# Modulation vectors computed up front by TensorE, or summed up by VectorE inside the other stages

## The chip, the cores and the metric

The kernel runs on one core of one Trainium2 chip. The metric is the time of one execution on the device in microseconds (us). The numbers of the trace come from one profiled execution, whose span is counted from its first instruction to its last.

## What is computed

Two transformer layers over 256 latent tokens `x` and 256 context tokens `ctx`, width D = 1024, everything in float32. Each layer first makes six modulation vectors of length D for each of two streams, one from the vector `c` (latent) and one from `c_ctx` (context):

```python
for i in range(DEPTH):                                   # 2 layers
    mod_l = (silu_c @ mod_w[i] + mod_b[i]).reshape(B, 1, N_MOD, D_MODEL)     # mod_w[i]: 1024 x 6144
    mod_c = (silu_cc @ mod_w[i] + mod_b[i]).reshape(1, N_MOD, D_MODEL)
    sh1, sc1, gt1, sh2, sc2, gt2 = [mod_l[:, :, s] for s in range(N_MOD)]
    u_l = rmsnorm(lat, norm_g[i, 0]) * (1 + sc1) + sh1
    ...  # layer 0: mLSTM mixer, layer 1: HGRN2 mixer; y_l
    lat = lat + gt1 * rmsnorm(y_l, norm_g[i, 1])
    u_l = rmsnorm(lat, norm_g[i, 2]) * (1 + sc2) + sh2
    lat = lat + gt2 * rmsnorm(ffn(u_l), norm_g[i, 3])    # layer 0: dense SwiGLU, layer 1: 8 experts, top 2
    ...  # layer 0 does the same for the context stream with csh1 ... cgt2
```

Shift and scale 1 are needed at the start of a layer, gate 1 only after the mixer, shift and scale 2 before the feed-forward part, gate 2 at the end. One layer's `mod_w` has 25 MB, so the 24 loads of 2 MB for both layers move 50 MB.

## The kernel before

The program is a list of stages, `order`. Each is one block with its own instruction stream for each engine, and all engines meet in a barrier at its end, so the times of the stages add up. The stages are: `setup` (small vectors, masks), `modulation(0)`, `norm_in` n0 (squares, scaling, 32 transposes of the tokens, then shift and scale), `mlstm_in` (projections), `mlstm_heads` (16 turns: 8 heads, 2 directions), `mixer_out`, `norm_in` n1, `feed_forward`, `modulation(1)`, `norm_in` n2, `hgrn_in` (projections), `hgrn_state`, `hgrn_pairs`, `hgrn_values`, `mixer_out`, `norm_in` n3, `routing`, `experts`, `finish`.

Weights come through `WeightStream`, a ring of `RING` slots of 2 MB. SyncE (SP) issues the load for unit n once the unit RING before it has been read for the last time (`release`). All waits of an engine are taken in the order of its instructions, so an instruction that waits holds back all that stand behind it on that engine.

Matrix products are made with each float32 operand split in two parts: ScalarE (ACT) copies a piece of 128x1024 weights to the high part, VectorE (DVE) subtracts to get the low part (`split_high`, `split_low`), and TensorE (PE) makes three matmuls of each pair. In `mlstm_in`, `hgrn_in` and `feed_forward` the pieces are double-buffered: piece p+2 is split once TensorE has done piece p. A piece in `mlstm_in` or `feed_forward` is 24 matmuls of 512 columns. In `mlstm_in` the first eight pieces (r = 0 to 7) each have a convolution of three VectorE instructions behind their split (the lines with `junk`), and after r = 3 `scan` has six instructions.

`modulation` reads `mod_w` through the same ring in 12 units of 512 columns. Each is split by ScalarE and VectorE, multiplied by TensorE with the four columns `c_parts` as the stationary operand (16 matmuls of 512 columns a unit), and the row is then either turned into columns (`mod_cols`, used as factors for each partition) or spread over the partitions (`gate`). Nothing else of the program runs beside it.

In `mlstm_heads`, for each turn n, `weigh(n)` has four VectorE instructions into `u_area`, which wait for ScalarE's exponentials; GpSimd then masks, and TensorE's `values(n)` (20 matmul records) follows. `finish(n)` is four VectorE instructions behind them. For each new head (even n) TensorE's `scores` waits until the `weigh` of the odd turn before it is done, and the exponentials wait for the `spread_m` behind `scores`.

## Time and profile before

| | before |
|---|---|
| median of 3 runs | 2219.05 us (2218.1 to 2224.69) |
| span of the profiled execution | 2219.4 us |
| TensorE busy | 1969.2 us, 89% |
| VectorE busy | 1394.1 us, 63% |
| ScalarE busy | 1112.6 us, 50% |
| DMA | 409.11 MB, mean 184 GB/s |

The busy shares are means over stages that are limited by different things. Since a barrier ends each stage, the profile is read stage by stage: first how long each takes and which engine fills it, then what one operation costs in it. The barriers of the trace put the stages at 18.3 to 120.0 us (`modulation(0)`), 120.0 to 135.4 (n0), 135.4 to 290.0 (`mlstm_in`), 290.0 to 392.4 (`mlstm_heads`), 392.4 to 469.8 (`mixer_out`), 485.4 to 863.0 (`feed_forward`), 863.0 to 956.0 (`modulation(1)`) and 972.5 to 1175.9 (`hgrn_in`).

### The profile page before, as it was taken

How to read it: one execution, taken by the hardware profiler on the slowest of the kernel's cores; microseconds unless marked ns; L12 is line 12 of the kernel's file. 1: busy time of each engine (PE TensorE's matmuls, PEld its weight loads, DVE VectorE, ACT ScalarE, POOL GpSimd, SP SyncE). 2: the span in 40 equal slices, each digit the busy share in tenths (PEclk: the TensorE clock that was granted, in tenths of full speed). 3: DMA queues.
4: the chain of work that ended last, by engine and by line, in shares of the span. 5: the costliest groups of instructions: out<-in, count | busy, mean ns of one | idle time of the engine just before them, and what ended most of it. 6: DMA issues, size and time to landing. Idle time of an engine off the chain costs nothing. (4 is left out here: it accounts for less than half of the span.)

```text
span 2219.4 us, 26725 instructions
## 1 busy us (share of the span) xinstructions
PE 1969.2 (89%) x10092; PEld 1615.5 (73%) x10092; DVE 1394.1 (63%) x1531; ACT 1112.6 (50%) x1244; POOL 110.5 (5%) x117
## 2 busy tenths in 40 slices
PE   5979988659999997869996675999999999999996
PEld 1247866548888874248895665989899898989895
DVE  5545234553233336745545844888888888888887
ACT  5433332343232225643234434677777777777765
POOL 1000012000000000000004800000000000000000
PEclk9879999879999998979998786999999999999998
DMA  9612210113232314822240004999999999999994
GB/s 328 233 60 104 76 39 1 38 38 114 76 113 76 114 57 172 310 88 94 76 152 1 1 1 149 323 348 324 345 329 348 325 348 319 354 320 336 335 331 175
DMA packets 254248, 409.11 MB, mean 184 GB/s; under 512 B 6575, under 2 KB 160327, under 8 KB 254055
## 3 DMA queue, kind: packets, MB, share of 16 engines
q1 hardware_dynamic: 254184, 408.23, 52.8%
q8 instruction: 43, 0.70, 0.1%
q14 instruction: 21, 0.17, 0.0%
HBM read 407.16 MB, written 1.05 MB: 184 GB/s over the span
## 5 line engine op out<-in xcount | busy, mean ns | idle before, releaser
L2002 DVE TENSOR_TENSOR w_low<-e_ring,w_high 128x1408 fp32r<-128x1408 f32 (+2 forms) x384 | 617.4, 1622 | 102.6 <-ACT w_high L1939 99.4
L1939 ACT ACTIVATE w_high<-e_ring 128x1408 fp32r<-128x1408 f32 (+2 forms) x384 | 528.7, 1382 | 214.7 <-PE ps L1852 212.2
L1850 PE MATMUL ps<-w_high,list_h 128*128 128x352 f32 x1024 | 338.1, 330 | 17.7 <-DVE w_low L2002 16.3
L1852 PE MATMUL ps<-w_high,list_l 128*128 128x352 f32 x1024 | 330.1, 322 | 0.0
L1851 PE MATMUL ps<-w_low,list_h 128*128 128x352 f32 x1024 | 329.3, 322 | 0.0
L1217 DVE TENSOR_TENSOR fw_low<-ring,fw_high 128x1024 fp32r<-128x1024 f32 x66 | 80.9, 1225 | 233.8 <-ACT fw_high L1183 233.8
L1850 PEld LDWEIGHTS ps<-w_high,list_h 128*128 128x128 f32 x1024 | 192.9, 188 | 26.4 <-DVE w_low L2002 25.5
L1183 ACT ACTIVATE fw_high<-ring 128x1024 fp32r<-128x1024 f32 x66 | 70.0, 1060 | 254.7 <-PE ps L1136 168.1
L1851 PEld LDWEIGHTS ps<-w_low,list_h 128*128 128x128 f32 x1024 | 193.7, 189 | 0.3
L1852 PEld LDWEIGHTS ps<-w_high,list_l 128*128 128x128 f32 x1024 | 192.9, 188 | 0.0
L1850 PE MATMUL ps<-w_high,hid_h 128*128 128x512 f32 x352 | 140.4, 399 | 5.4 <-DVE hid_l L2068 5.4
L1134 PE MATMUL ps<-u_high,fw_high 128*128 128x512 f32 x352 | 137.7, 391 | 6.7 <-DVE fw_low L1217 6.7
L1852 PE MATMUL ps<-w_high,hid_l 128*128 128x512 f32 x352 | 137.5, 391 | 0.0
L1136 PE MATMUL ps<-u_high,fw_low 128*128 128x512 f32 x352 | 137.4, 390 | 0.0
L1135 PE MATMUL ps<-u_low,fw_high 128*128 128x512 f32 x352 | 137.4, 390 | 0.0
L1851 PE MATMUL ps<-w_low,hid_h 128*128 128x512 f32 x352 | 137.3, 390 | 0.0
L387 ACT ACTIVATE u_high<-ring 128x1024 fp32r<-128x1024 f32 x96 | 98.5, 1050 | 65.7 <-PE ps L359 42.5
L419 DVE TENSOR_TENSOR u_low<-ring,u_high 128x1024 fp32r<-128x1024 f32 x96 | 111.5, 1218 | 9.5 <-ACT u_high L387 9.3
L594 DVE TENSOR_TENSOR h_part<-ring,h_part 128x1024 fp32r<-128x1024 f32 x40 | 49.0, 1225 | 79.0 <-ACT h_part L588 78.9
L588 ACT ACTIVATE h_part<-ring 128x1024 fp32r<-128x1024 f32 x40 | 42.3, 1057 | 100.9 <-PE ps L1320 100.9
L358 PE MATMUL ps<-u_high,c_parts 128*4 128x512 f32 x192 | 84.6, 441 | 6.9 <-DVE u_low L419 6.9
L359 PE MATMUL ps<-u_low,c_parts 128*4 128x512 f32 x192 | 85.0, 443 | 0.0
(323 smaller groups left out, 3631.7 us busy)
## 6 DMA issues: line engine op xcount, KB each, us to landing
e_ring<-in_e_w_gu_dram SPq DMA_DIRECT2D x128, 1408.0 KB, 8.0
ring<-in_mod_w_dram SPq DMA_DIRECT2D x24, 2048.0 KB
e_ring<-in_e_w_down_dram SPq DMA_DIRECT2D x32, 1536.0 KB, 7.2
...
```

The source lines that it names most:

```text
L358: nc.tensor.matmul(k.ps[0:4, n % 2, :], k.c_parts[:, c, :], part(k.u_high, q)[:, m, :], start=False, stop=False)
L359: last = nc.tensor.matmul(k.ps[0:4, n % 2, :], k.c_parts[:, c, :], part(k.u_low, q)[:, m, :], start=False, stop=(c == KD - 1))
L387: nc.scalar.activation(part(k.u_high, q), raw(n, q), ACT.Copy).then_inc(high_done, 1)
L419: nc.vector.tensor_tensor(part(k.u_low, q), raw(n, q), part(k.u_high, q).bitcast(F32), ALU.subtract).then_inc(low_done, 1)
L1134: nc.tensor.matmul(k.ps[:, bank, :], wh[:, m, :], k.u_high[:, m, :], start=(m == 0), stop=False)
L1135: nc.tensor.matmul(k.ps[:, bank, :], wh[:, m, :], k.u_low[:, m, :], start=False, stop=False)
L1136: last = nc.tensor.matmul(k.ps[:, bank, :], wl[:, m, :], k.u_high[:, m, :], start=False, stop=(m == KD - 1))
L1850: nc.tensor.matmul(out, high[:, f, :], w_high[:, c, :], start=(f == 0), stop=False)
L1851: nc.tensor.matmul(out, high[:, f, :], w_low[:, c, :], start=False, stop=False)
L1852: last = nc.tensor.matmul(out, low[:, f, :], w_high[:, c, :], start=False, stop=(f == total - 1))
L1939: nc.scalar.activation(piece(k.w_high, p), raw(p), ACT.Copy).then_inc(S.high_done, 1)
L2002: nc.vector.tensor_tensor(piece(k.w_low, p), raw(p), piece(k.w_high, p).bitcast(F32), ALU.subtract).then_inc(S.low_done, 1)
```

## The change

The two `modulation` stages, `setup` and n0 are gone from the list. One stage `opening` takes the place of the first three: it loads only the 8 MB of `mod_w` for shift 1 and scale 1 of layer 0 (four units of 2 MB, each into an area of its own), multiplies them unsplit in float32 (8 matmuls of 512 columns a unit, with the two columns `c_cols` as the stationary operand) and makes the norm of the tokens beside that.

The other ten of the twelve vectors (`MODS`) are made by a class `Background`. Their `mod_w` rows come in 80 items of 128x1024 (0.5 MB) through a small ring of two slots. For each item and stream VectorE has one `scalar_tensor_tensor` (`op`): accumulator = item x one column of `c` + accumulator. That is 128 instructions: 32 in `mlstm_in` (two a step at r = 5 to 12 and 16 to 23), 16 in `mlstm_heads` (one a turn), 64 in `feed_forward` (one a step), 16 in `hgrn_in` (one a step at 16 steps). TensorE then adds up over the 128 partitions (`sum`): for a gate 2 or 4 float32 matmuls of 512 columns with `ones` as the stationary operand, for a shift or scale 8 or 16 matmuls of one column with a 128x128 piece of the accumulator as the stationary operand. VectorE takes the result from PSUM (`take`).

The space comes from the weight ring, which has two slots where it had three. `feed_forward` keeps two PSUM banks free for the sums, so that its chunks rotate over three pairs of banks (before: four), and its loop over groups is written out. `hgrn_in` rotates over seven banks (before: eight). The core of the diff:

```diff
-RING = 3
+RING = 2
 SLOT = KD * HALF
+BG_RING = 2
@@ WeightStream.send @@
-                sp.dma_start(self.aux(n, place) if isinstance(place, int) else place(self.slot(n)), source).then_inc(self.loaded[n % RING], 16)
+                sp.dma_start(place(self.slot(n)), source).then_inc(self.loaded[n % RING], 16)
@@ plan_stream @@
-    def add_mod(layer):
-        start(f"mod{layer}")
-        for n in range(2 * N_MOD):
-            parts = [(wide, columns(a["mod_w"][layer], n * HALF, HALF)),
-                     (0, row(a["mod_b"][layer], n * HALF))]
-            if n // 2 in (2, 5):
-                gain = a["norm_g"][layer, 1 if n // 2 == 2 else 3]
-                parts.append((32, row(gain, (n % 2) * HALF)))
-            s.add(*parts)
-
-    add_mod(0)
...
-    add_mod(1)
@@ new @@
+class Background:
...
+    MODS = ((0, 2), (0, 3), (0, 4), (0, 5), (1, 0), (1, 1), (1, 2), (1, 3), (1, 4), (1, 5))
...
+    def load(self, sp, i):
+
+        q, c = i // KD, i % KD
+        layer, m = self.MODS[q]
+        if c == 0:
+            if q in self.CLEARED:
+                sp.wait_ge(self.cleared, self.CLEARED[q])
+            if q:
+                sp.wait_ge(self.used, self.ops_through((q - 1) * KD))
+            sp.dma_start(self.bias_rows[q][0:1, :], self.k.a["mod_b"][layer:layer + 1, m * D:(m + 1) * D]).then_inc(self.bias_in, 16)
+        if i >= BG_RING:
+            sp.wait_ge(self.used, self.ops_through(i - BG_RING))
+        sp.dma_start(self.slot(i), self.k.a["mod_w"][layer, c * P:(c + 1) * P, m * D:(m + 1) * D]).then_inc(self.loaded[i % BG_RING], 16)
...
+    def op(self, dve, i, n):
+
+        q, c = i // KD, i % KD
+        streams = self.streams(q)
+        j = streams[n]
+        if n == 0:
+            dve.wait_ge(self.loaded[i % BG_RING], 16 * (i // BG_RING + 1))
+        if c == 0:
+            if n == 0:
+                dve.wait_ge(self.bias_in, 16 * (q + 1))
+                if q in self.ACC_BEFORE:
+                    dve.wait_ge(self.summed, self.first_step[self.ACC_BEFORE[q] + 1])
+        else:
+            dve.wait_ge(self.used, self.ops_through(i - 1) - len(streams) + n + 1)
+        self.nc.vector.scalar_tensor_tensor(out=self.acc[q][j], in0=self.slot(i), scalar=self.k.c_cols[:, c, j:j + 1],
+                                            in1=self.bias_rows[q] if c == 0 else self.acc[q][j],
+                                            op0=ALU.mult, op1=ALU.add).then_inc(self.used, 1)
+
+    def item(self, dve, i):
+        for n in range(len(self.streams(i // KD))):
+            self.op(dve, i, n)
...
+    def sum(self, pe, q, n, bank, taken):
+
+        k, streams = self.k, self.streams(q)
+        pe.wait_ge(self.used, self.first_op[q + 1])
+        if taken:
+            pe.wait_ge(self.taken, taken)
+        if self.is_gate(q):
+            j, half = streams[n // 2], n % 2
+            last = self.nc.tensor.matmul(k.ps[:, bank, :], k.ones[:, :], self.acc[q][j][:, half * HALF:(half + 1) * HALF],
+                                         start=True, stop=True)
+        else:
+            for j in streams:
+                for c in range(KD):
+                    last = self.nc.tensor.matmul(k.ps[:, bank, 2 * c + j:2 * c + j + 1], self.acc[q][j][:, c * P:(c + 1) * P],
+                                                 k.ones[:, 0:1], start=True, stop=True)
+        last.then_inc(self.summed, 1)
...
@@ opening: SyncE @@
+            unit(0)
+            unit(1)
             sp.dma_start(k.resid[:, 0:2, :], a["ctx"][0].rearrange("(t p) d -> p t d", p=P)).then_inc(k.x_in, 16)
             sp.dma_start(k.resid[:, 2:4, :], a["x"][0].rearrange("(t p) d -> p t d", p=P)).then_inc(k.x_in, 16)
+            unit(2)
+            unit(3)
+            k.stream.send(sp, RING)
...
@@ opening: TensorE @@
+            pe.wait_ge(c_ready, 1)
+            for n in range(FIRST):
+                if n >= 2:
+                    pe.wait_ge(row_copied, n - 1)
+                pe.wait_ge(first_in[n], 32)
+                for c in range(KD):
+                    last = nc.tensor.matmul(k.ps[0:2, 2 + n % 2, :], k.c_cols[:, c, :], staged[n][:, c, :],
+                                            start=(c == 0), stop=(c == KD - 1))
+                    if c == 3 and n:
+                        turn_row(n - 1)
+                last.then_inc(row_ready, 1)
...
@@ mlstm_in @@
+    items_at = {r: r - 5 if r < 13 else r - 8 for r in (*range(5, 13), *range(16, 24))}
+    loads_at = {r: r - 3 if r < 13 else r - 6 for r in (*range(5, 13), *range(16, 24))}
...
+                if r == 14:
+                    for n, bank in enumerate((5, 6, 7, 0)):
+                        bg.sum(pe, 0, n, bank, 0)
...
+                if r in items_at:
+                    bg.item(dve, items_at[r])
...
@@ mlstm_heads @@
+            k.bg.sum(pe, 1, 0, 7, 0)
...
                 if n:
                     finish(n - 1)
+                else:
+                    k.bg.take(dve, 1, 0, 7)
+                k.bg.op(dve, 16 + n // 2, n % 2)
...
@@ mixer_out @@
+                k.bg.take(dve, last_mod, 0, 0)
+                k.bg.scale(dve, last_mod)
             for n in range(n_t):
                 dve.wait_ge(squared, n + 1)
...
@@ feed_forward @@
+    SUMS = {(1, 2): (3, ((0, 6), (1, 7)), 0), (1, 4): (3, ((2, 6), (3, 7)), bg.first_step[3] + 2),
+            (1, 10): (4, ((0, 6),), bg.first_step[4]), (2, 2): (5, ((0, 6),), 0), (2, 10): (6, ((0, 6), (1, 7)), bg.first_step[6])}
...
-                    bank = 2 * (q % 4) + side
+                    bank = 2 * (q % 3) + side
...
+                    if (g, p) in SUMS:
+                        m, steps_banks, taken = SUMS[g, p]
+                        pe.wait_ge(y_added, (g + 1) * 8)
+                        for n, bank in steps_banks:
+                            bg.sum(pe, m, n, bank, taken)
...
-                            pe.wait_ge(mult_done, g * F_GROUP + (2 + max(q for q in range(c) if q % 4 == i) + 1))
+                        if f == 0 and i < 3:
+
+                            pe.wait_ge(mult_done, g * F_GROUP + (2 + max(q for q in range(c) if q % 3 == i) + 1))
...
+                at = g * per + p
+                if at < 2 * two_ops:
+                    bg.op(dve, 24 + at // 2, at % 2)
+                elif at < 2 * two_ops + one_op:
+                    bg.op(dve, at, 0)
...
@@ hgrn_in @@
-    BANKS = 8
+    BANKS = 7
+    items_at = {p: 62 + p if p < 10 else 60 + p for p in (*range(2, 10), *range(12, 20))}
...
+            bg.sum(pe, 7, 0, 7, 0)
             for p in range(4 * units):
                 u, q = p // 4, p % 4
+                if p == 12:
+                    bg.sum(pe, 8, 0, 7, bg.first_step[8])
+                elif p in (22, 23):
+                    bg.sum(pe, 9, p - 22, 7, bg.first_step[9] + p - 22)
...
@@ order @@
-            lambda: setup(k),
-            lambda: modulation(k, 0),
-            lambda: norm_in(k, "n0", 0, range(NT), u_cols=k.u_raw, arrived=(k.x_in, 32)),
+            lambda: opening(k),
             lambda: mlstm_in(k),
...
             lambda: feed_forward(k),
-            lambda: modulation(k, 1),
```

`take` is one VectorE instruction a bank, 128x512 for a gate and 128x16 or 128x8 for a shift or scale; `scale` is one of 128x16. In `SUMS` the sums stand behind the pieces p = 2, 4 and 10 of the second group and 2 and 10 of the third.

How the instructions stand, at three places. First SyncE's queue at the program's start, before (`ring` and `ex` are the slots and bias rows of `modulation`, `resid` the tokens):

```order
L204 DMA w_router<-in_e_w_router_dram 128x8x8
L205 DMA b_router<-in_e_b_router_dram 1x8
L100 DMA ring<-in_mod_w_dram 128x8x512
L100 DMA ex<-in_mod_b_dram 1x512
L100 DMA ring<-in_mod_w_dram 128x8x512
L100 DMA ex<-in_mod_b_dram 1x512
L100 DMA ring<-in_mod_w_dram 128x8x512
L100 DMA ex<-in_mod_b_dram 1x512
L208 DMA resid<-in_ctx_dram 128x2x1024
L209 DMA resid<-in_x_dram 128x2x1024
```

and in the changed kernel:

```order
L321 DMA junk<-in_c_ctx_dram 8x128
L322 DMA junk<-in_c_dram 8x128
L319 DMA u_area<-in_mod_w_dram 128x4x512 x2
L319 DMA first_unit_60<-in_mod_w_dram 128x4x512 x2
L325 DMA resid<-in_ctx_dram 128x2x1024
L326 DMA resid<-in_x_dram 128x2x1024
L319 DMA bg_area<-in_mod_w_dram 128x4x512 x2
L319 DMA big<-in_mod_w_dram 128x4x512 x2
L96 DMA ring<-in_m_w_in_dram 128x8x32
L96 DMA ring<-in_m_w_in_dram 128x8x512
```

The small vectors that stood ahead of the first `mod_w` load have gone to ScalarE's queue, the tokens stand between the units, and the weights of `mlstm_in` follow in the same stage. Second, VectorE in `mlstm_heads`, from the `finish` of an odd turn over the `weigh` of the next odd turn (`ex<-ps,den` ends a `finish`), before:

```order
L916 TENSOR_TENSOR den<-ps,e_cols 128x4
L917 SCALAR_TENSOR_TENSOR den<-ps,den 128x4
L919 RECIPROCAL den<-den 128x4
L922 TENSOR_TENSOR ex<-ps,den 128x512
L906 SCALAR_TENSOR_TENSOR u_area<-ps,ex 128x512 x2
L906 SCALAR_TENSOR_TENSOR u_area<-ps,ex 128x128
L906 SCALAR_TENSOR_TENSOR u_area<-ps,ex 128x256
L916 TENSOR_TENSOR den<-ps,e_cols 128x4
```

and in the changed kernel:

```order
L1003 TENSOR_TENSOR den<-ps,e_cols 128x4
L1004 SCALAR_TENSOR_TENSOR den<-ps,den 128x4
L1006 RECIPROCAL den<-den 128x4
L1009 TENSOR_TENSOR ex<-ps,den 128x512
L232 SCALAR_TENSOR_TENSOR bg_area<-bg_area,c_cols 128x1024
L993 SCALAR_TENSOR_TENSOR u_area<-ps,ex 128x512 x2
L993 SCALAR_TENSOR_TENSOR u_area<-ps,ex 128x128
L993 SCALAR_TENSOR_TENSOR u_area<-ps,ex 128x256
L1003 TENSOR_TENSOR den<-ps,e_cols 128x4
```

An `op` (`bg_area<-bg_area,c_cols`) stands between `finish` and the next `weigh`, in this turn and in every other. Third, VectorE at the border from `mlstm_heads` to `mixer_out`, before:

```order
L826 UNCONDITIONAL_BRANCH
L994 UNCONDITIONAL_BRANCH
L1004 TENSOR_REDUCE head_sum<-big 128x8 x4
L1008 RECIPROCAL head_sum<-head_sum 128x8
L1010 TENSOR_TENSOR tok<-tok,head_sum 128x1024
L1008 RECIPROCAL head_sum<-head_sum 128x8
```

and in the changed kernel:

```order
L913 UNCONDITIONAL_BRANCH
L1084 UNCONDITIONAL_BRANCH
L269 COPY mod_cols<-ps 128x16
L282 SCALAR_TENSOR_TENSOR mod_scale<-mod_cols,vcol 128x16
L1097 TENSOR_REDUCE head_sum<-big 128x8 x4
L1101 RECIPROCAL head_sum<-head_sum 128x8
L1103 TENSOR_TENSOR tok<-tok,head_sum 128x1024
```

`take` and `scale` of the last vector of layer 0 stand ahead of the four reductions; `take` waits for 16 matmuls of one column, which stand first in TensorE's part of the stage.

## Rows read from the trace of the kernel before

**Rows 1.** Busy time by stage: start:end, length, each engine (instructions), granted clock, DMA share, GB/s.

```profile
core 0: us, PE busy (x) PEld busy (x) DVE busy (x) ACT busy (x) POOL busy (x), PEclk, DMA share, GB/s
18.30:120.00 101.70, 89.66 (x304) 27.73 (x304) 64.31 (x70) 54.84 (x60) 0.00 (x0) 0.86 0.76 273
135.40:290.00 154.60, 148.71 (x616) 113.59 (x616) 59.80 (x73) 52.83 (x66) 0.00 (x0) 0.97 0.28 96
290.00:392.40 102.40, 84.70 (x416) 61.26 (x416) 46.44 (x128) 29.79 (x65) 20.07 (x24) 0.92 0.00 1
485.40:863.00 377.60, 360.97 (x1584) 298.13 (x1584) 137.41 (x154) 108.22 (x135) 3.49 (x1) 0.98 0.27 92
863.00:956.00 93.00, 80.98 (x296) 25.38 (x296) 61.43 (x66) 54.99 (x60) 0.00 (x0) 0.89 0.77 271
972.50:1175.90 203.40, 192.60 (x1168) 167.99 (x1168) 106.38 (x124) 70.28 (x86) 4.12 (x1) 0.97 0.28 99
```

**Rows 2.** The same view of a stretch in which the ring's loads were outstanding.

```profile
24.00:40.00 16.00, 15.26 (x65) 5.18 (x64) 11.96 (x14) 11.88 (x14) 0.00 (x0) 1.00 1.04 394
```

**Rows 3.** TensorE's timeline: start, length, line, names, shapes, count; float32 matmuls at three places.

```profile
18.42 1.86 PE L353 MATMUL ps<-ex,first_rows 1*4 1x512 f32 x2 [12.12 <-PEq L187]
...
28.92 1.05 PE L332 MATMUL ps<-pair_sum,ex 4*128 4x2 f32 x8
...
338.79 1.98 PE L853 MATMUL ps<-ex,ident 16*128 16x512 f32 x4
```

**Rows 4.** VectorE's timeline in n0: its half of shift and scale.

```profile
131.39 3.71 DVE L484 TENSOR_SCALAR big<-ps,mod_scale,mod_cols 128x256 f32<-128x256 f32 x8 [2.41 <-PE ps L492]
```

**Rows 5.** VectorE's timeline in the residual of `feed_forward`, `scalar_tensor_tensor` of 128x1024.

```profile
854.90 1.28 DVE L529 SCALAR_TENSOR_TENSOR tok<-tok,rstd,gate 128x1024 f32<-128x1024 f32 x1
```

**Rows 6.** Timelines of VectorE and TensorE in `mlstm_in`, about the eighth piece.

```profile
195.84 1.23 DVE L594 TENSOR_TENSOR m_part<-ring,m_part 128x1024 fp32r<-128x1024 f32 x1 [1.72 <-ACT m_part L588]
...
203.71 0.75 DVE L781 SCALAR_TENSOR_TENSOR junk<-ps,vcol,junk 128x510 f32<-128x510 f32 x1
...
204.51 0.50 PE L674 MATMUL ps<-m_part,u_high 128*128 128x512 f32 x1 [0.82 <-DVE junk L781]
```

**Rows 7.** Timelines of VectorE, then TensorE, for turns of `mlstm_heads`.

```profile
333.39 1.81 DVE L906 SCALAR_TENSOR_TENSOR u_area<-ps,ex 128x512 f32<-128x512 f32 x4
...
340.76 1.68 DVE L906 SCALAR_TENSOR_TENSOR u_area<-ps,ex 128x512 f32<-128x512 f32 x4 [2.84 <-ACT ex L890]
...
324.95 2.84 PE L844 MATMUL ps<-big 64*128 64x512 f32 x8
...
333.61 2.47 PE L864 MATMUL ps<-big,u_area 128*128 128x129 f32 x20 [1.48 <-DVE ex L922]
336.01 2.84 PE L844 MATMUL ps<-big 64*128 64x512 f32 x8
...
340.70 3.96 PE L864 MATMUL ps<-big,u_area 128*128 128x129 f32 x20
...
348.53 0.69 PE L844 MATMUL ps<-big 64*128 64x512 f32 x1
```

**Rows 8.** VectorE's timeline at the start of `mixer_out`.

```profile
393.62 4.60 DVE L1004 TENSOR_REDUCE head_sum<-big 128x8 f32<-128x1024 f32 x4 [2.76 <-ACT big L981]
```

**Rows 9.** `feed_forward` where the down projection starts: TensorE, VectorE, then the waits of TensorE.

```profile
577.31 0.39 PE L1151 MATMUL ps<-fw_high,fh_high 128*128 128x512 f32 x1
577.54 0.39 PE L1152 MATMUL ps<-fw_low,fh_high 128*128 128x512 f32 x1
...
579.75 0.68 DVE L1223 TENSOR_TENSOR ex<-ex,ps 128x512 f32<-128x512 f32 x1
...
PE ps L1151 <- DVE ex L1223: 1.6, 1, 1.6
```

**Rows 10.** `hgrn_in` behind a unit's last piece: VectorE, then ScalarE.

```profile
1014.06 1.22 DVE L594 TENSOR_TENSOR h_part<-ring,h_part 128x1024 fp32r<-128x1024 f32 x1
...
1016.75 1.06 ACT L588 ACTIVATE h_part<-ring 128x1024 fp32r<-128x1024 f32 x1 [4.56 <-PE ps L1320]
```

467 lines of the change are left out of this document (266 added, 201 removed).

## The prediction

> **What bounds the kernel now.** I read the busy times by stage first [rows 1]. The two `modulation` stages last 101.7 and 93.0 us and take 0.76 and 0.77 of the DMA engines' time at 273 and 271 GB/s. Inside them the loads wait for ring slots: with loads always outstanding the same queue moves 394 GB/s [rows 2]. So these stages are held by the chain of split, matmul and release, and nothing else of the program runs beside them. The four stages that receive the new work look different. In `feed_forward` TensorE is busy 361.0 of 377.6 us and VectorE only 137.4; in `mlstm_in` it is 148.7 against 59.8 of 154.6, in `hgrn_in` 192.6 against 106.4 of 203.4. DMA is at 0.27 to 0.28 in these three. TensorE bounds them, and VectorE and the DMA engines have room. In `mlstm_heads` no engine is full (TensorE 84.7, VectorE 46.4 of 102.4): that is a chain of waits, where added VectorE work costs what it puts on the chain, whatever the idle share. From there I went to the timelines, one engine after another, at the places where new instructions stand.
>
> **What is taken away.** `modulation(1)` goes whole: 93.0 us. `setup`, `modulation(0)` and n0 end at 135.4 us [rows 1], and `opening` takes their place, so its end is what counts. Its loads: 4.2 MB for units 0 and 1, 2.1 MB of tokens, 4.2 MB for units 2 and 3. At 394 GB/s [rows 2] from about 3 us (my choice: the first load is issued after two small ones) the units are there at 8.3, 13.6, 24.3 and 29.6 us. TensorE: a float32 matmul has two records. Four records of 512 columns take 1.98 us in `mlstm_heads`, about 0.45 each without the last one's tail, so 0.9 a matmul; the first two of the program took 1.86 us together, 0.93 each [rows 3]. With two matmuls at the slow price unit 0 costs 3.7 + 6 x 0.9 = 9.1 us and ends at 17.4; each later unit costs 7.2 plus 1.05 for turning the row before it (eight records of two columns [rows 3]): 25.7, 33.9, 42.1. So TensorE, not DMA, bounds the stage after its first unit. The norm of the tokens is done by then, under the matmuls. Behind them stand 20 transposes and the last row (28 records x 0.13 = 3.7), the add and the factor (0.4, estimate), shift and scale as in n0, 3.71 us [rows 4], and the barrier: 50 us. Gain 85.4 us. If the loads start at 2 and nothing is slow it is 46; if every matmul went at 0.93 a record, 32 x 1.86 instead of 32 x 0.93 would end it near 78.
>
> **What the 128 `op` cost.** None is in the trace; the nearest row is the same instruction with the same shape in the residual, 1.28 us [rows 5]. 128 x 1.28 = 164 us of VectorE. That is nearly all that the change saves, so it decides where they lie.
> - `feed_forward`, 64: the piece rhythm is 24 matmuls x 0.23 = 5.4 us [rows 9]. VectorE has 1.23 for the low part and 0.68 behind it a step; with 1.28 it is 3.2 of 5.4. The low part stands ahead of the `op`. Cost 0. Without that cover 82 us.
> - `mlstm_in`, 32 in pairs of 2.56: from r = 8 on a step is 1.23 + 2.56 = 3.8 of 5.5, hidden. At r = 5 and 6 the convolutions (2.3) are there too, and the chain goes VectorE, ScalarE, VectorE: VectorE's wait before the next split was 1.72 us [rows 6], so 2.56 - 1.72 = 0.85 a step is added, twice ahead of the eighth convolution. That one ended at 204.46 and TensorE, which had waited 0.82 us for it, went on at 204.51 [rows 6]. Cost 1.7 us. The three items behind the last split (7.7 us) lie under two pieces.
> - `mlstm_heads`, 16: behind the odd turns VectorE waits 2.84 us for ScalarE before `weigh` [rows 7], which hides 1.28. Behind the even turns `weigh` starts at once (333.39 us), and `scores` of the next head, at 336.01, waits for its end, ScalarE for `scores`, and the next `weigh` (340.76) for ScalarE. There the full 1.28 is on the chain: 7 x 1.28 = 9.0. The first turn has TensorE's 16 one-column matmuls ahead of `values(0)` and VectorE waits for them: between 0 and 6.3 us (below); I take 3, the middle. Together 12.0.
> - `hgrn_in`, 16: behind a unit's last piece the next low part ended at 1015.28, and TensorE needed it at 1016.75 [rows 10]. The margin of 1.47 just covers 1.28. Cost 0; up to 1.3 at each of three places if a little more is added.
>
> **What the sums cost.** They stand in TensorE's order, where TensorE bounds. A gate matmul is 0.9. For one column with a 128x128 operand the nearest rows are the two-column records, 1.05 / 8 = 0.13, and the records of 129 columns, 2.47 / 20 = 0.12 quick and 3.96 / 20 = 0.20 slow [rows 3, 7]. The bounds are 0.05 and 0.20; I take 0.13 where TensorE is busy, 0.20 where it comes from idling.
> - `mlstm_in`: 4 gate matmuls, 3.6; with the 1.7 above 5.3.
> - `mixer_out`: TensorE would idle there, but VectorE's `take` stands ahead of the reductions. 32 records x 0.20 = 6.3 from 392.5 and 0.4 for the two small instructions: the reductions start at 399.2 where they started at 393.62 [rows 8]. Everything of the stage's start hangs on them: 5.6.
> - `feed_forward`: 6 gate matmuls 5.4, 64 records 8.4. The three pairs of banks add this: the second block of a down projection's first piece waits for the last product. The piece starts at 577.31, the product ends at 580.43 [rows 9], the second block would start 6 x 0.23 = 1.4 in. So 1.7 us of waiting in each of two groups; the third group already had 1.6 [rows 9] and keeps about 0.4. Net 2.2. Together 16.0.
> - `hgrn_in`: 8 + 8 one-column matmuls 4.2 (5.3 if the first eight are slow), 2 gate matmuls 1.8: 6.3.
>
> **The ring of two slots** costs nothing by itself. A slot is free when the unit's fourth piece is split, and its next unit is first wanted nearly five pieces later, about 25 us. A unit takes 2.1 MB / 394 = 5.3 us, and a 0.5 MB item beside it 1.3. An item is wanted two steps, 11 us, after its issue, and with a unit ahead of it takes 6.6 and the latency. If that cover were gone, each of the 33 later units would add its lateness.
>
> **The sum:** 2219.4 - 85.4 - 93.0 + 5.3 + 12.0 + 5.6 + 16.0 + 6.3 = 2086.2. The profiled execution (2219.4) lies 0.35 us above the median of the runs (2219.05), so I give 2086.
>
> **The rivals.**
> A. *The background lane is late.* All its steps are in the engines' orders: a late item holds VectorE's next split and so TensorE. For it: SyncE issues items and units in one queue, and waits for VectorE between them. Against it: the 4 us of slack above. If each of 30 units made one item a microsecond late past its cover, +30: 2116; half that is as likely. 2104 to 2140, chance 0.10.
> B. *TensorE runs slow for longer.* In `mlstm_heads` the same 20 records take 2.47 or 3.96 us; the pair of turns from 324.95 took 11.06 us and that from 336.01 12.52 [rows 7]; the stage's granted clock is 0.92 [rows 1]. I find three slow pairs of eight. The change adds idle time in front of `scores`, and if all were slow, 5 x 1.5 = 7.5 us more; the opening could take another 10 to 25 us. 2094 to 2120, chance 0.10. By the Trainium skill ("TensorE: Matmul & The Clock Gate", section HAM oscillation) a TensorE that idles between bursts drops to half clock and starts each burst cold; the two prices of one group agree with a factor near two. By that rule the `heads` stage would end 7.5 us later than in my sum, 2094.
> C. *Slower.* VectorE's `op` are not covered in the TensorE-bound stages, for example because each adds a hand-over between split and matmul. The 120 that I count as hidden (or all but 1.7 us of them) cost 154 us at full price: 2240. It decides from 133 / 120 = 1.1 us a piece. Against it speak the 2.2 us free in each 5.4 us step. Chance 0.03.
> D. *The ring starves.* It undoes the gain from 133 / 33 = 4 us a unit; against it, 25 us of notice for 5.3 of transfer. Chance 0.01 for anything above 2140.
>
> **How the numbers follow.** The sum holds with 0.76, within 2068 to 2104: the one-column records at 0.05 give -8, the opening at 46 -4, no cost at the first turn -3, on the other side 10 for the opening and small stalls. The range for 8 in 10 reaches into A and B: 2066 to 2116. No change within 0.3% (6.7 us, about what a measurement of this kernel can tell) would need a chance meeting of A and C: 0.01. Slower 0.03, faster 0.96.
>
> **What would show it.** Right: a first stage that ends near 50 us with TensorE busy from 8 us on; no wait of `op` for a load over 1 us; `feed_forward` near 394 us with two waits of about 1.7 us on the down projection; pairs of turns near 12.3 us; reductions in `mixer_out` about 6.8 us after the barrier. Wrong: waits of the split copies for loads, of `op` for loads, or TensorE waiting for the low part in each step. The prediction falls most easily with the opening, whose matmuls I price from rows of other stages, and with the one-column matmuls, which no row shows.

## The result and the profile after

| | before | after |
|---|---|---|
| median of 4 runs each, on the same chip | 2218.57 us (2215.56 to 2224.69) | 2109.80 us (2109.03 to 2115.88) |
| ratio, with its 95% interval | | 0.9514 (0.9494 to 0.9534) |
| span of the profiled execution | 2219.4 us | 2114.2 us |

The change takes 109 us away, where 133 were forecast: 24 us above the forecast of 2086 us and inside its range of 2066 to 2116. The forecast was made against one profiled execution, so I compare execution with execution first: 2219.4 - 2114.2 = 105.2 us, where the sum said 133.2. Missing: 28 us. The sum was to hold within 2068 to 2104 us; the rest of the range belonged to the rivals, and the result lies there. The profiled execution is the longest of the four (2115.88 us; the others have 2109.03 to 2109.99), so its trace shows some 6 us more than the median. A second set of runs of the same changed kernel (the control below) had a median of 2102.87 us. What lies between these two is one of the findings.

The busy times by stage of the changed kernel, with the columns of [rows 1]: `opening`, `mlstm_in`, `mlstm_heads`, `mixer_out`, `feed_forward`, `hgrn_in`.

```profile
0.00:50.40 50.40, 38.43 (x132) 13.21 (x132) 10.26 (x33) 14.93 (x26) 10.18 (x27) 1.00 0.73 255
50.40:214.40 164.00, 155.03 (x624) 115.13 (x624) 100.33 (x109) 52.81 (x66) 0.00 (x0) 0.97 0.45 151
214.40:342.90 128.50, 110.55 (x448) 80.11 (x448) 65.18 (x145) 29.86 (x65) 20.04 (x24) 0.73 0.10 29
342.90:427.80 84.90, 59.69 (x256) 49.43 (x256) 43.44 (x54) 26.88 (x41) 0.00 (x0) 0.78 0.15 50
442.20:839.20 397.00, 377.58 (x1660) 308.96 (x1660) 217.68 (x227) 104.25 (x132) 4.40 (x2) 0.98 0.42 145
855.00:1070.00 215.00, 200.25 (x1204) 172.53 (x1204) 127.19 (x145) 70.30 (x86) 5.22 (x2) 0.96 0.43 145
```

The first stage ends at 50.4 us where three stages ended at 135.4: 85 us gained, as forecast. `modulation(1)` is gone. The other lines show what is paid back: `mlstm_in` +9.4, `mlstm_heads` +26.1, `mixer_out` +7.5, `feed_forward` +19.4; n2 and `hgrn_in` together have 230.8 us where they had 219.9, +10.9. n1 is 1.2 shorter, what comes after is 0.7 longer. VectorE is busy for 160 us more in the four stages that have the `op`, and these stages, with `mixer_out` and n2, grow by 73 in all. `mlstm_heads` stands out, and its granted clock says where to look: 0.73, before 0.92 [rows 1].

The opening on TensorE's timeline (start, length, line, shapes, count, idle time ahead):

```profile
10.06 8.79 PE L427 MATMUL ps<-u_area,c_cols 128*2 128x512 f32 x16
18.69 3.60 PE L427 MATMUL ps<-first_unit,c_cols 128*2 128x512 f32 x8
22.22 1.05 PE L417 MATMUL ps<-ident,ex 2*128 2x2 f32 x8
...
45.91 1.53 PE L435 MATMUL ps<-ident,tok 128*128 128x128 f32 x12
```

TensorE works from 10.1 to 47.4 us. The first unit has 16 records in 8.79 us, partly slow (forecast 9.1), each later half unit 3.60, so 7.2 a unit, as priced from [rows 3]. TensorE waits for no weight load; it starts at 10.1 us and not earlier because it waits 2.7 us for a row of `mod_b`, until 9.26.

The end of `mlstm_in` and the start of `mlstm_heads`, timelines of SyncE, VectorE and TensorE:

```profile
201.95 0.38 SPq L96 DMA_DIRECT2D ring<-in_m_w_out_dram  x1
204.35 0.33 SPq L209 DMA_DIRECT2D bg_area<-in_mod_w_dram  x1
...
211.22 2.48 DVE L232 SCALAR_TENSOR_TENSOR bg_area<-bg_area,c_cols 128x1024 f32<-128x1024 f32 x2 [4.51 <-DMA bg_area<-in_mod_w_dram]
...
214.50 4.93 PE L930 MATMUL ps<-big 64*128 64x512 f32 x8 [3.79 <-PEq L694]
...
223.06 6.99 PE L253 MATMUL ps<-ones,bg_area 128*128 128x1 f32 x32
229.91 4.65 PE L950 MATMUL ps<-big,u_area 128*128 128x129 f32 x20
234.49 3.34 PE L930 MATMUL ps<-big 64*128 64x512 f32 x8
```

The last item (0.5 MB) is issued at 204.35 us, 2.4 us behind a unit of 2 MB for `m_out`, which nobody wants before the stage after next. VectorE waits 4.51 us for the item, TensorE has been done since 210.7 and waits 3.79 us at the barrier. Then TensorE is slow: `scores` takes 4.93 us for the eight records that took 2.84 in [rows 7], the 32 one-column records 6.99 us, `values` 4.65, where this first group had 4.08 before and a quick one has 2.47. From `scores` to `scores` the first pair of turns took 20.0 us, the next two 16.6 and 19.3 (before 11.2, 11.1, 12.7), and only from 270 us on are the numbers those of before. The granted clock is 0.52, 0.59 and 0.62 in the three 20 us slices from 214.4 to 274.4 and 0.91 in the next.

`mixer_out` starts with the same 32 records, on TensorE, and VectorE waits for them:

```profile
343.02 6.96 PE L253 MATMUL ps<-ones,bg_area 128*128 128x1 f32 x32 [3.02 <-PEq L913]
...
350.02 0.17 DVE L269 COPY mod_cols<-ps 128x16 f32<-128x16 f32 x1 [8.69 <-PE ps L253]
...
350.32 4.59 DVE L1097 TENSOR_REDUCE head_sum<-big 128x8 f32<-128x1024 f32 x4
```

The reductions begin 7.4 us after the barrier, where they began 1.2 us after it [rows 1, 8].

`feed_forward`: the waits of TensorE (engine, line, who released it; us, times, longest), then, from TensorE's timeline, one of its one-column sums, and windows of 4 us about it (columns as above):

```profile
PE ps L1276 <- DVE ex L1345: 3.6, 3, 1.6
PE ps L1276 <- DVE gate L266: 0.7, 1, 0.7
```

```profile
644.51 3.63 PE L253 MATMUL ps<-ones,ex 128*128 128x1 f32 x32
```

```profile
644.00:648.00 4.00, 4.00 (x35) 3.88 (x35) 2.14 (x3) 1.58 (x2) 0.00 (x0) 1.00 1.00 402
648.00:652.00 4.00, 4.00 (x13) 3.18 (x13) 0.89 (x1) 0.00 (x0) 0.00 (x0) 0.57 0.49 202
652.00:656.00 4.00, 4.00 (x19) 3.34 (x18) 0.00 (x0) 0.67 (x1) 0.00 (x0) 1.00 0.00 0
```

The same windows behind the stage's other sum of 32 such records, which starts at 738.9 us:

```profile
740.00:744.00 4.00, 4.00 (x30) 3.73 (x30) 3.02 (x3) 0.74 (x2) 0.00 (x0) 1.00 1.09 363
744.00:748.00 4.00, 4.00 (x20) 3.28 (x19) 0.00 (x0) 0.00 (x0) 0.00 (x0) 1.00 0.60 206
```

No line says that TensorE waits for an `op`: the 64 instructions are hidden. The three waits for the last product are there. The windows show something else: behind 32 one-column records the clock is 0.57 for 4 us, 13 records instead of 19, although TensorE was busy without a break. The second sum has no such stretch. Over the eleven profiled executions in this study that have both sums whole, the first is followed by a low stretch in all, the second in six.

In `hgrn_in` one wait is new:

```profile
PE ps L248 <- DVE gate L266: 3.2, 1, 3.2
```

The second half of the last gate sum stands one piece behind the first, has the same bank, and waits for `take` of the first half, which VectorE reaches late in its step.

### The profile page after: what moved, and what is told of

It is laid out like the page before. It is cut to its first block and busy times, and to the rows that moved or that the text cites. A ratio compares the mean times of both kernels' runs of the same rounds, so it can differ in the third digit from the quotient of the medians.

```text
span 2114.2 us, 25835 instructions
## 1 busy us (share of the span) xinstructions
PE 1896.8 (90%) x9774; PEld 1614.1 (76%) x9774; DVE 1428.8 (68%) x1543; ACT 1001.4 (47%) x1125; POOL 113.2 (5%) x120
## 5 line engine op out<-in xcount | busy, mean ns | idle before, releaser
L2008 PE MATMUL ps<-w_high,list_h 128*128 128x352 f32 x1024 | 338.2, 330 | 18.0 <-DVE w_low L2160 16.4
L232 DVE SCALAR_TENSOR_TENSOR bg_area<-bg_area,c_cols 128x1024 f32<-128x1024 f32 x93 | 117.6, 1278 | 5.1 <-DMA bg_area<-in_mod_w_dram 5.0
L652 ACT ACTIVATE h_part<-ring 128x1024 fp32r<-128x1024 f32 x40 | 42.3, 1058 | 111.9 <-PE ps L1469 111.9
L2008 PEld LDWEIGHTS ps<-w_high,hid_h 128*128 128x128 f32 x352 | 66.1, 188 | 25.4 <-DVE w_low L2160 11.9
L1252 PEld LDWEIGHTS ps<-u_high,fw_high 128*128 128x128 f32 x352 | 67.1, 191 | 22.3 <-issue 8.6
L1253 PEld LDWEIGHTS ps<-u_low,fw_high 128*128 128x128 f32 x352 | 67.1, 191 | 14.6 <-issue 0.7
```

The costliest lines, as they stand in the source:

```text
L232: self.nc.vector.scalar_tensor_tensor(out=self.acc[q][j], in0=self.slot(i), scalar=self.k.c_cols[:, c, j:j + 1], in1=self.bias_rows[q] if ...
L1252: nc.tensor.matmul(k.ps[:, bank, :], wh[:, m, :], k.u_high[:, m, :], start=(m == 0), stop=False)
L1253: nc.tensor.matmul(k.ps[:, bank, :], wh[:, m, :], k.u_low[:, m, :], start=False, stop=False)
L2008: nc.tensor.matmul(out, high[:, f, :], w_high[:, c, :], start=(f == 0), stop=False)
```

## The experiments

Two theories for `mlstm_heads`: **A**, the late item and the idle time that it makes ahead of the stage cause the slow start; **B**, the one-column sum does, and what stands behind it. Stage lengths below are from barrier to barrier in each kernel's profiled execution. The first four kernels ran on one chip (before: median 2218.41 us), the next four on one (2216.5), the last four on one (2216.69).

**The control**, the changed kernel without an edit.

> The changed kernel itself, once more, as the control of this group. All theories: 2108 to 2111 us, 0.951 of the kernel before; mlstm_in 164.0, mlstm_heads 128.5, mixer_out 84.8, feed_forward 397.0 us. If mlstm_heads comes out more than 5 us away from 128.5 here, its slow stretch varies by itself, and the other three of the group are read stage by stage with that spread.

Measured: 2102.87 us (2101.26 to 2108.79), ratio 0.948 (0.9451 to 0.9509). `mixer_out` 84.8 and `feed_forward` 397.0 are the same to 0.1 us, `mlstm_in` has 162.3, but `mlstm_heads` has 116.0 instead of 128.5 us. Its idle time ahead is the same 3.75 us, `scores` again slow (4.15), the sum again 6.99; only the clock comes back after the first pair (0.58 until 233 us, 0.91 in the next 20 us) instead of after the third. So 12.5 of the 26 us are not the same from one execution to another. These two traces are the longest execution of one set and the shortest of the other, and I don't know whether both sets ran on one chip, so no run here says how much of the 12.5 is the chip's. The control also shows undisturbed what `op` costs, VectorE and TensorE in a pair of turns:

```profile
280.49 2.84 PE L930 MATMUL ps<-big 64*128 64x512 f32 x8 [0.36 <-DVE u_area L993]
...
290.56 1.27 DVE L232 SCALAR_TENSOR_TENSOR bg_area<-bg_area,c_cols 128x1024 f32<-128x1024 f32 x1
290.79 2.47 PE L950 MATMUL ps<-big,u_area 128*128 128x129 f32 x20 [1.48 <-DVE ex L1009]
...
293.62 0.69 PE L930 MATMUL ps<-big 64*128 64x512 f32 x1 [0.36 <-DVE u_area L993]
```

The `op` of the even turn (290.56) does push `weigh` back, to 291.75. But TensorE is in `values` until 293.26 anyway, and `scores` starts 0.36 us later. The price is 0.36 to 0.43 us a pair (11.5 and 13.1 us where before had 11.06 and 12.67), not 1.28. Only behind the last head, where no `scores` follow, is it nearly full: the wait ahead of the last `values`, first before, then in the control, is 1.2 us longer.

```profile
385.41 4.11 PE L864 MATMUL ps<-big,u_area 128*128 128x129 f32 x20 [1.99 <-DVE ex L922]
...
321.02 4.64 PE L950 MATMUL ps<-big,u_area 128*128 128x129 f32 x20 [3.18 <-DVE ex L1009]
```

**Item before unit.**

```diff
             for r in range(5, 24):
-                if r % 4 == 1:
+                if r % 4 == 1 and r < 21:
                     s.send(sp, u0 + 4 + r // 4)
                 if r in loads_at:
                     bg.load(sp, loads_at[r])
+            s.send(sp, u0 + 9)
```

> The second 2 MB unit of m_out is sent behind the last item loads of mlstm_in instead of ahead of the last one. Theory A (the late item ends mlstm_in 3 us late and makes TensorE stand idle for 3.8 us, and this idle time is what starts mlstm_heads at the low clock): the 4.5 us wait of op for its load goes, mlstm_in ends 3 us earlier (161), and mlstm_heads is back near 110 us; in all 15 to 20 us less, 2091 to 2095. Theory B (the clock stays low because the one-column sum and the wait behind it keep TensorE thinly used at the start of the stage): mlstm_in 3 us less, mlstm_heads the same 128, in all 3 us less, 2107.

Measured: 2099.38 us (2096.01 to 2105.24), ratio 0.9455 (0.9422 to 0.9487). VectorE's wait falls to 1.51 us, TensorE's to 1.26, `mlstm_in` has 159.8 us, 2.5 less than the control. The totals of the two kernels can't be told apart (their executions overlap), the stages can. `mlstm_heads` begins quick, but slows down:

```profile
210.30 2.82 PE L931 MATMUL ps<-big 64*128 64x512 f32 x8 [1.26 <-PEq L694]
213.05 2.62 PE L940 MATMUL ps<-ex,ident 16*128 16x512 f32 x4
215.60 6.99 PE L253 MATMUL ps<-ones,bg_area 128*128 128x1 f32 x32
222.44 4.65 PE L951 MATMUL ps<-big,u_area 128*128 128x129 f32 x20
```

`mlstm_heads` 116.6 us, the control 116.0: A's 15 to 20 us are not there. The first pair is 2.2 us shorter (16.7 after 18.9), which is the quick `scores` and `spread_m`, and the second 3.3 longer. In this pair of traces A is right about the first two groups and not about the rest; more traces of the same code follow below.

**A short sum.** This kernel and the next leave out seven eighths of the sum at the start of `mlstm_heads`; they route the tokens otherwise, and their last stages take some 840 us longer for that reason alone (whole 2944.01 and 2943.20 us). Only the stages up to `hgrn_in` are read.

```diff
-    def sum(self, pe, q, n, bank, taken):
+    def sum(self, pe, q, n, bank, taken, chunks=KD):
...
-                for c in range(KD):
+                for c in range(chunks):
...
-            k.bg.sum(pe, 1, 0, 7, 0)
+            k.bg.sum(pe, 1, 0, 7, 0, chunks=1)
```

> Sum of the second vector at the start of mlstm_heads with 1 of 8 chunks (2 matmuls, 4 records, instead of 16 and 32): seven eighths of that sum are left out. By itself this takes away 7 x 4 x 0.22 = 6.1 us of slow TensorE ahead of the first values. Theory B (thin matmuls keep the clock low): the slow stretch ends with it, mlstm_heads is near 110 us, 18 less. Theory A (idle time ahead of the stage): the stage still starts slow, and only the 6 us are saved, mlstm_heads 122.

Measured: `mlstm_heads` 111.9 us, 4.1 less than the control. The first pair has 14.5 us instead of 18.9, the others are as in the control. Against 128.5 us, where the expectation started, neither theory's number can be read any more; against the control the sum's own time is all that goes.

**Both edits.**

> Both edits: second unit of m_out behind the last items, and only 1 of 8 chunks of the sum at the start of mlstm_heads (seven eighths of that sum left out). If A or B alone is the cause, this equals the one that works, plus the other one's own 3 or 6 us: A 2086 to 2090, B 2086 to 2090. If the stage is still slow for its first three heads (mlstm_heads 120 or more), neither is the cause, and the clock falls for what the stage itself does.

Measured: `mlstm_heads` 109.3 us. TensorE's timeline:

```profile
212.38 2.81 PE L931 MATMUL ps<-big 64*128 64x512 f32 x8 [1.43 <-PEq L694]
215.13 1.98 PE L940 MATMUL ps<-ex,ident 16*128 16x512 f32 x4
217.03 0.61 PE L253 MATMUL ps<-ones,bg_area 128*128 128x1 f32 x4
220.59 4.67 PE L951 MATMUL ps<-big,u_area 128*128 128x129 f32 x20 [2.95 <-POOL u_area L1038]
225.19 3.03 PE L931 MATMUL ps<-big 64*128 64x512 f32 x8
```

Four one-column records take 0.61 us here, but `values` behind them is slow again (4.67), now after 2.95 us of waiting for GpSimd's mask. So even with a short sum one slow group stands there, as it does before (4.08 behind a wait of 2.42). The mask itself takes 1.70 us here, beside an `op` on VectorE, where it takes 0.64 before and in the control. The first pair in the four kernels: 18.9 (control), 16.7 (item first), 14.5 (short sum), 12.8 (both); before 11.2. In these four executions the edits give about 2 and 4 us, and they add. But one execution of each can't carry the 2 us: in the five later kernels that also send the item first the first pair has 18.2, 13.9, 13.9, 13.9 and 17.2 us, and with the late item and the whole sum it has 20.0 in after and 20.4 in the kernel with short column sums in `feed_forward`. Sending the item first thus goes with a shorter first pair in every trace (13.9 to 18.2 against 18.9 to 20.4). How much of the rest of the slow time, up to 12.5 us, it takes away is open.

**Both `op` of an item at odd turns** (with item before unit), to test the 1.28 us a pair of the prediction.

```diff
-                k.bg.op(dve, 16 + n // 2, n % 2)
+                if n % 2:
+                    k.bg.item(dve, 16 + n // 2)
```

> On top of the late second unit of m_out: both op of an item stand behind the odd turns of mlstm_heads, none behind the even ones. The prediction's own term (1.28 us on the chain of every even turn): seven pairs of turns 1.28 shorter, the stage 9 us less, about 107. The trace of after instead (weigh of an even turn ends under the values of the turn before; scores wait 0.36 us for it): 0.36 to 0.43 a pair, the stage 3 us less, about 113; if the second op behind an odd turn delays weigh there (2 x 1.28 = 2.56 against 2.8 of wait for ScalarE), nothing or a loss of up to 2. One low-clock pair more or less is 1.6 us and is read apart, from the length of the scores and values records.

Measured: 2093.18 us (2087.14 to 2101.36), ratio 0.9433 (0.9413 to 0.9453), `mlstm_heads` 114.1 us with a slow second pair. Pairs without a slow group take 11.1 us, with one 12.7, where the control has 11.5 and 13.1: 0.4 a pair, as the trace of after said, and the number of before. The prediction's 9 us would have given pairs of 10.2. The wait ahead of the last `values` is back at 1.98 us, so the last head gives 1.2 us more.

**`take` behind the normalisation in `mixer_out`** (with item before unit).

```diff
-            if last_mod is not None:
-                k.bg.take(dve, last_mod, 0, 0)
-                k.bg.scale(dve, last_mod)
             for n in range(n_t):
                 dve.wait_ge(squared, n + 1)
...
+            if last_mod is not None:
+                k.bg.take(dve, last_mod, 0, 0)
+                k.bg.scale(dve, last_mod)
             for h in range(HEADS):
                 dve.wait_ge(turned, h + 1)
```

> On top of the late second unit of m_out: take and scale of the last vector in mixer_out stand behind the normalisation instead of ahead of the first reduction. Theory (VectorE waits for TensorE's 32 one-column records of 0.22 us at the head of the stage, and everything hangs on its reductions): the reductions start 1.2 us after the barrier instead of 7.4, mixer_out 78.6 instead of 84.8, in all 6.2 us less than e1_item_first, 2093. Rival (the sum delays the transposes on TensorE, or a factor is wanted later than the normalisation, and VectorE's wait only moves): mixer_out stays over 83.

Measured: 2089.77 us (2085.87 to 2091.02), ratio 0.9424 (0.9406 to 0.9443). `mixer_out` 79.1 us, 5.0 less than in the kernel with item first alone (84.1), and the reductions start 1.2 us after the barrier:

```profile
322.70 4.60 DVE L1095 TENSOR_REDUCE head_sum<-big 128x8 f32<-128x1024 f32 x4 [2.75 <-ACT big L1072]
```

The reductions start 6.2 us earlier and the stage is 5.0 shorter, so most of its price of 7.5 us was the wait in front of them; 1.7 us above before's 77.4 are left. The whole is lower than the 2093 us expected because of another stage: `mlstm_heads`, the same code as with item first (116.6), came out at 109.1 us.

**All reorderings.** The two above, odd turns, and these:

```diff
-                    for i in range(NT):
+                    for i in ((0, 3, 2, 1) if c == F_GROUP else (0, 1, 3, 2)) if f == 0 else range(NT):
...
-                elif p in (22, 23):
-                    bg.sum(pe, 9, p - 22, 7, bg.first_step[9] + p - 22)
+                elif p in (22, 24):
+                    bg.sum(pe, 9, (p - 22) // 2, 7, bg.first_step[9] + (p - 22) // 2)
```

> All reorderings together: m_out's second unit behind the last items; op at odd turns; take and scale behind the normalisation in mixer_out; in feed_forward the first piece of each down projection takes first the blocks whose banks come free first (token blocks 0, 3, 2, 1 for eight pieces, 0, 1, 3, 2 for six); in hgrn_in the second gate sum one piece later. Expected by the waits of after's trace: mlstm_in 161, heads 113 to 115, mixer_out 78.6, feed_forward 394 (three waits of 3.6 us in all gone), hgrn_in with n2 3.2 us less (227.5). In all 16 us less than e1_item_first: 2083. Rival: the waits are covered elsewhere (each by the split of the next piece or a later wait), and only mixer_out gains: 2092.

Measured: 2079.64 us (2077.18 to 2083.23), ratio 0.9388 (0.9373 to 0.9403), the lowest median of the study (the kernels with a filler and with another order of blocks, below, can't be told apart from it). `mlstm_in` 158.3, `mlstm_heads` 104.5, `mixer_out` 78.3 us, n2 and `hgrn_in` 226.2, where the wait of 3.2 us for the gate bank is gone. `feed_forward` did not follow: 399.3 instead of 394. Its waits of TensorE for the product are gone, but one for a gate product has grown:

```profile
PE ps L1278 <- DVE gate L266: 2.7, 1, 2.7
```

That is 1.6 us net, and the clock took more: three low stretches instead of one. The same `feed_forward` code without the edit had 397.0 to 400.9 us in the other traces, so the edit's own gain can't be read from the length. That the total comes near the 2083 us expected is in part luck: `mlstm_heads` gave 104.5 where 113 to 115 were expected, against the 5 us lost here.

**A filler matmul** on top of all reorderings.

```diff
+                if n % 2 and n > 1:
+                    pe.wait_ge(masked, n)
+                    nc.tensor.matmul(k.ps[:, 7, :], k.qk[0:64, 4, 0:P], k.qk[0:64, 0, :], start=True, stop=True)
                 if n:
                     values(n - 1)
```

> As e7_all, with one more float32 matmul of 512 columns (two records, 0.9 us) into a free bank ahead of the values of every even turn but the first of mlstm_heads, where TensorE idles 1.5 us. Theory B (TensorE drops to the low clock because it idles within the turns): the granted clock of the stage from its second pair on is 1.0, no values group takes 4.1 us, each of the three or more slow pairs is 1.6 us shorter: heads 5 us less than e7_all. Rival (the low clock comes from thin records and one idle stretch at the head of the stage, or the filler lies on the chain since the pair is held by TensorE's own work): heads the same or up to 7 x 0.5 = 3.5 us longer.

Measured: 2079.96 us (2077.21 to 2083.22), `mlstm_heads` 105.0 us where it was 104.5, granted clock 0.90 where it was 0.89. TensorE's timeline:

```profile
277.58 4.14 PE L951 MATMUL ps<-big,u_area 128*128 128x129 f32 x20
281.65 1.12 PE L967 MATMUL ps<-big 64*128 64x512 f32 x2
283.20 2.47 PE L951 MATMUL ps<-big,u_area 128*128 128x129 f32 x20 [0.43 <-DVE ex L1013]
```

The idle time ahead of the even turn's values fell from 1.48 to 0.43 us, and slow groups of 4.14 us are still there, in the same number of pairs (three). Taking this much of the idle time away doesn't bring the clock back; the run doesn't clear the idle time that is left.

**Before, with a ring of two slots** (`RING = 3` to `RING = 2`, nothing else).

> The kernel before with the weight ring of two slots instead of three, nothing else. The prediction's claim (a unit has 25 us of notice and needs 5.3): no change, within 0.3% of before, 2212 to 2223; no new wait of the split copies for a load. Rival D (the ring starves): from 4 us a unit it would cost 133 us; already 1 us a unit would give 2250.

Measured: 2240.22 us (2239.21 to 2241.49), ratio 1.0103 (1.0084 to 1.0122): 23.5 us slower, where I expected nothing. The windows of `modulation(0)`, `mlstm_in`, `mlstm_heads` and `modulation(1)`:

```profile
12.70:125.20 112.50, 89.77 (x304) 28.17 (x304) 64.55 (x70) 53.35 (x60) 0.00 (x0) 0.87 0.70 247
141.40:296.90 155.50, 149.62 (x616) 113.82 (x616) 59.80 (x73) 52.91 (x66) 0.00 (x0) 0.96 0.27 95
296.90:399.10 102.20, 84.48 (x416) 60.89 (x416) 46.47 (x128) 29.80 (x65) 20.06 (x24) 0.92 0.00 1
...
869.80:979.20 109.40, 88.51 (x296) 26.78 (x296) 62.13 (x66) 53.58 (x60) 0.00 (x0) 0.81 0.66 231
```

The two `modulation` stages have 10.8 and 16.4 us more (`setup` ends 5.6 earlier, with one load less to send), `mlstm_in` +0.9, `mlstm_heads` -0.2, n0 +0.8, n1 with `feed_forward` +0.1, n2 with `hgrn_in` -1.3, what comes after -3.9; the spans are 18 us apart. In the stages that the change keeps, two slots cost nothing, as the prediction said. This run has no items beside the ring; in the trace of after, which has them, no copy of ScalarE waits for a load in `mlstm_in`, `feed_forward` or `hgrn_in` either. The stages that wait for ring slots are the two that it removes, and the prediction had named them so. My expectation for this run forgot them.

**Every `op` twice** (the second adds zero times the slot).

```diff
+        self.again += 1
+        self.nc.vector.scalar_tensor_tensor(out=self.acc[q][j], in0=self.slot(i), scalar=0.0,
+                                            in1=self.bias_rows[q] if c == 0 else self.acc[q][j],
+                                            op0=ALU.mult, op1=ALU.add).then_inc(self.twice, 1)
+        dve.wait_ge(self.twice, self.again)
```

> The changed kernel with every op issued twice: ahead of each a second one of the same shape that adds zero times the slot, with a wait between the two; the result is the same, VectorE has 128 x (1.28 + about 0.1) = 177 us more. It asks how much cover there is left. If the cover is what the prediction counts (feed_forward 3.2 of 5.4 us a step busy): feed_forward within 5 of 397, since 4.6 still fits; mlstm_in, where a step then has 1.23 + 5.4 = 6.6 of 5.5, 1.1 x 14 steps and 2.7 at two convolutions more, 15 to 25 us; mlstm_heads 1.4 in even turns less nothing hidden, and nothing at odd ones, 8 x 1.4 = 11 us; hgrn_in 3 to 12. In all 30 to 55 us, 2135 to 2165. Rival C (op are not covered, each adds a hand-over): near 177 us more, 2280, most of it in feed_forward.

Measured: 2162.33 us (2158.66 to 2165.99), 59 us more than the control for some 160 us more work on VectorE (128 x 1.25). By stage: `mlstm_in` 174.9 (+12.6), `mlstm_heads` 151.4 (+35.4), `feed_forward` 408.4 (+11.4), `hgrn_in` 218.6 (+3.6).

```profile
226.50:377.90 151.40, 125.45 (x448) 86.37 (x448) 84.62 (x161) 30.07 (x65) 20.01 (x24) 0.68 0.08 25
477.30:885.70 408.40, 382.00 (x1660) 311.44 (x1660) 295.91 (x291) 104.25 (x132) 4.40 (x2) 0.97 0.41 141
```

In `feed_forward` 78 us more on VectorE cost 11 (at most 5 were expected): rival C is far off. In `mlstm_heads` 20 us cost 35 (11 were expected): all pairs after the first have 15.7 to 17.7 us instead of 11.5 and 13.1, and each has a slow group. That the total lies in the expected range is therefore chance. TensorE's timeline shows how the 35 divide:

```profile
263.24 3.83 PE L936 MATMUL ps<-big 64*128 64x512 f32 x8 [1.62 <-DVE u_area L999]
```

The wait ahead of `scores` is 1.62 us where it was 0.36: the second `op` of an even turn is on the chain with its full 1.26 us, since the first has used up the room. The other 3.5 of the 4.8 us a pair are matmuls at the low clock (granted 0.68, control 0.83). Here more idle time in a pair and more slow groups go together.

**Short column sums in `feed_forward`** (1 of 8 chunks of layer 1's shift and scale; seven eighths left out; read up to `hgrn_in`).

```diff
-                            bg.sum(pe, m, n, bank, taken)
+                            bg.sum(pe, m, n, bank, taken, chunks=1 if m in (4, 5) else KD)
```

> The changed kernel with the two column sums of feed_forward (the vectors of layer 1, shift and scale) over 1 of 8 chunks: seven eighths of them are left out, so that the routing of the last stages changes and only the stages up to the end of hgrn_in are read. 56 records of 0.11 go from TensorE's order: 6.2 us. If thin records also make the clock fall in the middle of a busy stage (in after's trace it is low from 648.0 to 652.0 us, behind one of them), that stretch goes as well, 2 us: feed_forward 388.5 to 389.5. Rival (the low stretch comes from something else): 390.8 and the low stretch is still there.

Measured: `feed_forward` 389.1 us, 7.9 less than the control's 397.0. Over its 389 us every slice of 10 us but the first and the last has a granted clock of 1.00; the control has 0.83 in the one with the low stretch, 627.7 to 637.7 us. 56 x 0.113 = 6.3 us are the records, the other 1.6 the clock. It is one execution, but the stage had 397.0 to 397.2 us in five others, and none of them was without that stretch.

**Another order of blocks.** `((2, 0, 3, 1) if c == F_GROUP ...` in the kernel with all reorderings.

> As e7_all, but the first piece of a down projection of eight pieces takes its token blocks in the order 2, 0, 3, 1. In e7_all the three waits of 3.6 us for the last product went, and the wait for a gate product rose from 0.7 to 2.7 us. With block 3 one block (1.4 us) later it falls to 1.3: 2078, at most 1.4 us less than e7_all, which this measurement can't tell apart; the trace can.

Measured: 2088.80 us (2076.51 to 2091.44), ratio 0.9403 (0.9377 to 0.943). The wait for the gate product is 2.7 us as before, so the edit does nothing. The executions lie up to 15 us apart: the profiled one has 165.1 us in `mlstm_in` where the kernel with all reorderings had 158.3. `mlstm_in` varies like that in other kernels too (158.3 to 167.6); the long ones have a granted clock of 0.78 to 0.88 in two slices of 10 us where others have 0.89 to 1.00, and TensorE then waits 3.2 us instead of 1.7 ahead of a bank. I can't say what chooses between them.

## Why the prediction was right where it was, and wrong where not

**The whole.** The mechanism is right: the two stages go, and most of the new VectorE work is hidden. The size is not as good as a result inside the range makes it look: the profile lies 28 us above the sum, outside the 2068 to 2104 us in which the sum was to hold, and one term that was too high hides one that was too low.

**What bounds the kernel, and what is taken away.** Right. Opening: forecast 50, measured 50.4; `modulation(1)` gone whole. Inside the opening small errors cancel: TensorE starts at 10.1 instead of 8.3 us, the later units take 7.9 instead of 8.25, and the last ends at 42.6 where 42.1 was forecast.

**The `op`.** Right in the large: 1.25 to 1.28 us each, hidden in `feed_forward` (no wait of TensorE for one) and `hgrn_in`. In `mlstm_heads` the term 7 x 1.28 = 9.0 was mis-sized: six waits ahead of `scores` cost 0.4 us each in the control, 2.5 together, and the last head, which the term left out, 1.2. The step that failed is "There the full 1.28 is on the chain". It followed `scores` <- `weigh` <- `op` on VectorE and overlooked TensorE's own order: [rows 7] has `values` from 333.61 to 336.08 us and `scores` at 336.01, so `weigh`, done at 335.20 (333.39 + 1.81), had some 0.8 us of slack. The run with both `op` at odd turns shows it. The sign "pairs of turns near 12.3 us" came true in the mean of the control's pairs, but by chance: that mean has one slow group more than before in it. In `mlstm_in` "Cost 1.7 us" was rather high (TensorE's wait behind the eighth convolution grew from 0.82 to 1.7 us, in other executions to 3.2) and had no late item in it: "the 4 us of slack above" fails at the one item behind a unit of 2 MB at the end of the stage, 4.51 us of wait and 2.5 of the stage (item before unit). That was rival A, in small.

**The first turn of `mlstm_heads`.** Forecast 3 us, "between 0 and 6.3". Measured 18.9 - 11.2 = 7.7 in the control and 8.8 in after: by the four kernels about 4 are the sum, 2 the slow start behind the idle time (one execution each, see above), and 1.6 stay with both edits: 1.1 for a mask that takes 1.70 us beside an `op` instead of 0.64, and 0.6 for a slower `values`. The records were priced right (6.3, measured 6.99, of which the mask's wait of 2.95 covers a part); "I take 3, the middle" is the step that failed, since it had the slow clock around the sum not in it. The two errors of the stage, 5.3 us too much on the chain and 4.7 too little at the start, nearly cancel in the control. Its 13.6 us against 12.0 are 7.7 + 2.5 + 1.2, one slow group of 1.6 us more than before, and 0.5 by which the last `values` is slower.

**Rival B.** Its effect came true in the execution that stands for after, not its form: it had every pair lose 1.5 us, and in fact the first three, low from end to end, took 8.8, 5.5 and 6.6 us more than before. Priced at 7.5 us, it was 12.5 (128.5 against 116.0). The two prices it compares differ by 1.6, since those groups are slow for a part only; a group low from end to end takes 4.65 us against 2.47, 1.9 times. Nearly half of the 28 us that the profile of after has above the sum is this, and it is not a property of the change alone: the same code of the stage had 128.5, 116.0 and 117.7 us behind the late item and 116.6 and 109.1 with the item first.

**The sums.** A record of one column took 0.113 us at the high clock (3.63 / 32) and 0.218 at the low one (6.99 / 32); 0.13 and 0.20 were forecast. By the Trainium skill ("TensorE: Matmul & The Clock Gate", section LDWEIGHTS) the time to load the stationary operand is its columns divided by 1.2 in ns, 107 ns for 128 columns; the quick row agrees, the slow one is twice that. `mixer_out`: forecast 5.6, measured 7.5; the reductions start 6.2 later, the other 1.3 is not assigned. `feed_forward`: forecast 16.0, measured 19.4; the records and the gate matmuls (7.2 + 5.7) are 0.9 below the forecast, the waits 4.3 - 1.6 = 2.7 against 2.2; what was missing is the low clock behind a thin sum (1.6 us by short sums), and about 2 us are not assigned. n2 and `hgrn_in`: forecast 6.3 (its two terms, 4.2 and 1.8, make 6.0), measured 10.9; missing is the gate sum that waits 3.2 us for its bank, and 1.4 are not assigned.

**The ring.** Right for the stages that stay.

**The sum again**, for the profiled execution, terms above forecast: opening +0.4, `mlstm_in` +4.1, `mlstm_heads` +14.1, `mixer_out` +1.9, `feed_forward` +3.4, n2 and `hgrn_in` +4.6, n1 and the rest -0.5: 28.0 us, from 2086.2 to 2114.2.
